# New places in the order for every step of the mixer stages MN, D and LG

## The reference

```
h = rmsnorm(x, norm1_w)
proj = h @ w_in          # mq mk mv mo mi mf nq kc vc ks vs kw vw ng gm gn
hm = mlstm_chunkwise(q, k, v, i_pre, logf)      # 4 heads
hm = rmsnorm(hm) * sigmoid(mo)
qn, kc_t, ks_t, kw_t = apply_rope(rmsnorm(...)) # 64 per head
kcmp = gelu(flat_k @ cmp_k_w1) @ cmp_k_w2       # blocks of 32 tokens, stride 16
vcmp = gelu(flat_v @ cmp_v_w1) @ cmp_v_w2
o_cmp, o_slc, o_win = nsa_branches(...)         # three softmax attentions
y = sigmoid(gm + b0) * (hm @ w_up_m) + sigmoid(gn + b1) * (on @ w_up_n)
x = x + y @ w_out
x = x + (gelu(conv(a)) * v) @ ffn_w_down        # a, v = split(rmsnorm(x) @ ffn_w_up)
```

## Time and profile before

| what | value |
|---|---|
| median of three runs | 2805.1 us (2800.53 to 2806.18) |
| profiled execution, span | 2803.7 us |
| PE busy | 2740.2 us, 98% |
| DVE, ACT, POOL busy | 65%, 46%, 18% |
| PE's share of the chain that ended last | 89% |
| MN, 98 to 420.5 us: PE busy of 322.5 | 315.75 us |
| D, 1281 to 1416 us: PE busy of 135 | 134.13 us |
| LG, 2191 to 2411 us: PE busy of 220 | 218.90 us |

### The profile page before, as it was taken

The page is one execution under the profiler, slowest core; times in us unless marked ns, Lnnn a source line. Parts: engine busy times, 40 slices in busy tenths (PEclk is TensorE's granted clock), DMA queues, the critical chain, the costliest instruction groups (busy, mean ns, idle before and its releaser), DMA issues.

```text
span 2803.7 us, 40660 instructions
## 1 busy us (share of the span) xinstructions
PE 2740.2 (98%) x15808; PEld 2348.4 (84%) x15808; DVE 1816.9 (65%) x2803; ACT 1288.7 (46%) x2190; POOL 516.9 (18%) x514
## 2 busy tenths in 40 slices
PE   8999999999999999999989999999999999899999
PEld 7787777888878898987778999889998787688988
DVE  7667666646467574756767566675765677774755
ACT  5445554322235353543644344543544686643533
POOL 1001332000003121101303212031120343131211
PEclk9999999999999999999999999999999999999999
DMA  5212104232223564631124565354653110234743
GB/s 177 66 61 93 42 27 151 90 98 98 90 83 91 142 159 129 169 109 53 31 94 134 127 166 133 122 140 113 177 130 101 42 34 28 83 96 135 191 113 113
DMA packets 112783, 296.53 MB, mean 106 GB/s; under 512 B 12624, under 2 KB 14672, under 8 KB 112336
## 3 DMA queue, kind: packets, MB, share of 16 engines
q1 hardware_dynamic: 90864, 250.80, 27.6%
q0 software_dynamic: 21152, 42.08, 9.1%
q10 hardware_dynamic: 576, 1.05, 0.1%
HBM read 291.78 MB, written 2.10 MB: 105 GB/s over the span
## 4 chain that ended last, share of the span: by engine, by line
PE 89%; DVE 6%; ACT 3%; issue 1%; POOL 0%; DMA 0%; SPq 0%; ACTq 0%; DVEq 0%; POOLq 0%
PE ps L510 87%; DVE WL L521 3%; PE ps L513 2%; ACT WH L518 1%; DVE SC L521 1%; ACT HH L518 1%; DVE X L521 1%; ACT SC L518 1%; DVE SC L533 0%; DVE HL L533 0%; POOL SC L528 0%; DMA WF<-wall 0%; DVE X2k L521 0%; DVE X2v L521 0%; DVE SM L539 0%
## 5 line engine op out<-in xcount | busy, mean ns | idle before, releaser
L521 DVE TENSOR_TENSOR WL<-WF,WH 128x1024 fp32r<-128x1024 f32 (+4 forms) x625 | 728.1, 1177 | 317.3 <-ACT WH L518 313.2
L518 ACT ACTIVATE WH<-WF 128x1024 fp32r<-128x1024 f32 (+4 forms) x625 | 581.2, 943 | 656.9 <-PE ps L510 623.0
L510 PE MATMUL ps<-HH,WH 128*128 128x512 f32 (+1 forms) x1104 | 443.5, 402 | 16.3 <-DVE HL L533 13.6
L510 PE MATMUL ps<-HH,WL 128*128 128x512 f32 (+1 forms) x1104 | 433.4, 393 | 0.0
L510 PE MATMUL ps<-HL,WH 128*128 128x512 f32 (+1 forms) x1104 | 433.1, 392 | 0.0
L510 PE MATMUL ps<-AH,WH 128*128 128x512 f32 x880 | 345.5, 393 | 19.4 <-DVE WL L521 15.6
L510 PE MATMUL ps<-AL,WH 128*128 128x512 f32 x880 | 343.3, 390 | 0.0
L510 PE MATMUL ps<-AH,WL 128*128 128x512 f32 x880 | 343.2, 390 | 0.0
L510 PE MATMUL ps<-B,WH 128*128 128x256 f32 x1632 | 299.8, 284 | 2.0 <-DVE WL L521 1.4
L521 POOL TENSOR_TENSOR SC<-SC 128x256 f32<-128x256 f32 (+2 forms) x92 | 108.2, 1182 | 983.6 <-DVE SC L533 978.7
L556 POOL DMA_DIRECT2D WF<-wall x136 | 128.8, 956 | 799.9 <-DMA WF<-wall 784.9
(11 more groups left out here) (322 smaller groups left out, 4770.7 us busy)
## 6 DMA issues: line engine op xcount, KB each, us to landing
WF<-wall SPq DMA_DIRECT2D x313, 512.0 KB, 3.8
WF<-wall SPq DMA_DIRECT2D x253, 256.0 KB, 3.0
WF<-wall POOLq DMA_DIRECT2D x136, 256.0 KB, 4.3
WF<-wall SPq DMA_DIRECT2D x40, 384.0 KB, 3.7
X<-xT POOLq DMA_DIRECT2D x8, 256.0 KB, 3.9
outT<-X POOLq DMA_DIRECT2D x8, 256.0 KB, 2.3
WF<-wall SPq DMA_DIRECT2D x4, 288.0 KB, 11.7
LT<-late POOLq DMA_DIRECT2D x1, 1152.0 KB, 5.6
```

What stands on the lines that cost most here:

```text
L510: return self.real.matmul(o, l, r, start=start, stop=stop, skip_group_check=True)
L518: return self.real.activation(o, i, func, bias=bias, scale=scale, accum_out=accum_out)
L521: return self.real.tensor_tensor(o, a, b, op) if self.real is not None else Uncounted()
```

## The change

Only the five dictionaries change: of 954 places in MN 926 differ, of 348 in D 334, of 825 in LG 798. No step is added or removed and none computes anything else. Five pairs of neighbouring weight pieces, of 625, swap places in the order in which they are fetched. The names that the prediction speaks of (the places of a stage are in the order of its keys; `source` in M has ks, kw, kc, nq0 and vc, four each; `take` and the others ks, kw, kc, nq0, and `take` also vc):

```
 M_TURNS = {
-    "source": (72, 80, 85, 86, 118, 125, 126, 147, 149, 155, 164, 165, 263, 267, 268, 269, 202, 235, 241, 253),
-    "take": (89, 152, 174, 273, 260),
-    "rot": (97, 182, 209, 275),
-    "sums": (116, 219, 234, 278),
-    "spread": (187, 236, 246, 287),
-    "done": (218, 256, 265, 316),
-    "x_made": (266, 270),
-    "x_first": (280, 282, 291, 293, 300, 303, 304, 311),
-    "x_bent": (306, 313),
-    "x_turned": (307, 320),
-    "product": (70, 145, 216, 255),
-    "h_sums": (122, 204, 225, 262),
-    "wf_low": (12, 49, 58, 101, 123, 179, 195, 274),
+    "source": (73, 80, 81, 82, 126, 129, 130, 136, 149, 150, 155, 161, 242, 248, 249, 254, 222, 224, 225, 243),
+    "take": (85, 142, 170, 267, 245),
+    "rot": (91, 173, 211, 265),
+    "sums": (138, 251, 214, 266),
+    "spread": (180, 269, 252, 301),
+    "done": (195, 290, 261, 311),
+    "x_made": (270, 246),
+    "x_first": (273, 274, 275, 281, 305, 306, 313, 314),
+    "x_bent": (292, 315),
+    "x_turned": (309, 316),
+    "product": (67, 121, 206, 244),
+    "h_sums": (109, 213, 258, 257),
+    "wf_low": (28, 69, 307, 107, 116, 187, 208, 276),
...
-    "f_part": (..., 213, 222, 264, 271),
+    "f_part": (..., 233, 259, 263, 264),
...
 D_TURNS = {
-    "made": (69, 73, 94, 131, 142, 151, 172, 177, 188, 191, 206, 239, 253, 262, 263, 296),
-    "raised": (90, 97, 102, 134, 146, 167, 179, 186, 202, 203, 217, 254, 264, 278, 295, 299),
+    "made": (82, 83, 97, 138, 148, 152, 166, 180, 193, 207, 211, 235, 257, 264, 265, 272),
+    "raised": (86, 101, 105, 140, 162, 163, 183, 184, 194, 215, 217, 262, 266, 268, 281, 296),
...
 L_TURNS = {
-    "source": (1, 6, 8, 9, 20, 43, 53, ...),
-    "take": (2, 7, 21, 26, ...),
-    "rot": (13, 19, 33, 57, ...),
+    "source": (1, 13, 5, 391, 23, 29, 56, ...),
+    "take": (3, 14, 10, 24, ...),
+    "rot": (2, 22, 18, 78, ...),
...
```

More of the change, by code:

```diff
@@ L292 @@
[L292 to L306, removed]
@@ L338 @@
[L338 to L343, removed]
@@ L344 @@
-    "half2": (534, 535, 722, 731, 839, 862, 950, 952),
-    "parts": (536, 802, 946, 953),
+    "source": (389, 390, 397, 400, 553, 554, 562, 564, 704, 705, 706, 707),
+    "ws_high": (250, 543, 683),
+    "ws_low": (147, 583, 744),
+    "take": (414, 568, 718),
+    "rot": (415, 597, 726),
+    "squares": (408, 586, 723),
+    "roped": (421, 602, 730),
+    "added": (445, 600, 743),
+    "sums": (418, 593, 748),
+    "root": (420, 594, 749),
+    "widen": (453, 601, 751),
+    "spread": (464, 610, 762),
@@ L346 @@
+    "product": (448, 465, 500, 506, 626, 634, 684, 688, 779, 781, 823, 830, 902, 910, 951, 953),
+    "half1": (517, 520, 710, 711, 857, 858, 948, 949),
+    "half2": (545, 546, 713, 728, 864, 866, 946, 947),
+    "parts": (549, 758, 950, 952),
 }
 D_TURNS = {
[L348 to L361, removed]
@@ new lines @@
+        153, 154, 164, 182, 187, 222, 224),
+    "ws_high": (15, 149, 40, 8, 62, 74, 143, 219),
+    "ws_low": (11, 298, 39, 9, 77, 116, 188, 233),
+    "take": (16, 30, 50, 75, 76, 111, 169, 230),
+    "rot": (19, 44, 81, 69, 78, 144, 185, 229),
+    "squares": (18, 37, 56, 66, 99, 110, 175, 227),
+    "roped": (32, 54, 87, 85, 96, 145, 186, 237),
+    "added": (24, 33, 79, 93, 130, 156, 197, 231),
+    "sums": (20, 38, 70, 72, 102, 115, 191, 232),
+    "root": (21, 45, 71, 73, 114, 137, 192, 234),
@@ new lines @@
+    "widen": (35, 43, 88, 84, 123, 151, 190, 238),
+    "spread": (42, 46, 117, 112, 135, 165, 228, 243),
+    "scaled": (58, 57, 129, 126, 150, 170, 236, 249),
+    "done": (53, 55, 131, 136, 168, 172, 245, 256),
+    "o_part": (59, 60, 104, 113, 128, 134, 212, 213, 250, 253, 255, 280, 293, 294, 331, 337),
+    "o_add": (61, 121, 141, 216, 260, 305, 312, 341),
+    "wo_high": (67, 108, 119, 196, 218, 263, 302, 306),
+    "wo_low": (48, 118, 132, 80, 254, 286, 311, 347),
+    "s_product": (2, 28, 0, 5),
@@ L423 @@
+    "product": (148, 216, 281, 315, 371, 425, 478, 511),
+    "half1": (169, 247, 296, 318, 408, 447, 485, 515),
+    "half2": (175, 245, 307, 328, 404, 460, 487, 525),
+    "parts": (265, 343, 479, 526),
 }
 G_TURNS = {
-    "source": (470, 471, 476, 477, 562, 564, 566, 575, 666, 671, 677, 678),
-    "ws_high": (467, 576, 659),
-    "ws_low": (488, 595, 783),
-    "take": (484, 583, 682),
-    "rot": (507, 592, 690),
-    "squares": (489, 587, 683),
-    "roped": (519, 601, 697),
-    "added": (527, 603, 709),
@@ L433 @@
-    "sums": (504, 590, 686),
-    "root": (505, 597, 700),
-    "widen": (506, 608, 701),
-    "spread": (526, 614, 708),
-    "scaled": (533, 627, 710),
-    "done": (545, 628, 715),
-    "o_part": (525, 535, 541, 542, 550, 551, 586, 600, 610, 611, 625, 650, 770, 799, 807, 813),
-    "o_add": (548, 560, 580, 609, 621, 668, 816, 819),
-    "wo_high": (485, 537, 556, 578, 615, 657, 681, 806),
-    "wo_low": (536, 558, 563, 591, 644, 702, 812, 814),
-    "made": (482, 508, 521, 522, 557, 582, 607, 624, 654, 684, 685, 707, 722, 748, 751, 768),
@@ L456 @@
-    "product": (623, 636, 695, 712, 759, 777, 810, 824),
-    "half1": (626, 637, 704, 743, 764, 796, 811, 820),
-    "half2": (634, 648, 705, 744, 766, 804, 815, 821),
-    "parts": (817, 818, 822, 823),
+    "source": (456, 469, 470, 473, 560, 561, 578, 579, 671, 672, 682, 685),
+    "ws_high": (423, 571, 661),
+    "ws_low": (458, 605, 662),
+    "take": (477, 584, 684),
+    "rot": (507, 586, 697),
+    "squares": (484, 588, 700),
+    "roped": (524, 601, 699),
+    "added": (527, 607, 693),
@@ L460 @@
+    "product": (602, 644, 694, 731, 755, 784, 805, 817),
+    "half1": (606, 632, 702, 737, 764, 785, 813, 822),
+    "half2": (630, 665, 709, 727, 781, 799, 811, 820),
+    "parts": (680, 812, 816, 823),
 }
```

274 lines of the change are left out of this document (139 added, 135 removed).

## The result

| | before | after |
|---|---|---|
| median | 2805.6 us (2800.5 to 2807.6, 4 runs) | 2787.4 us (2785.7 to 2789.0, 4 runs) |
| profiled execution, span | 2803.7 us | 2784.7 us |

The ratio is 0.994 (95% interval 0.9928 to 0.9951): 14 to 20 us less. I forecast 6 us less, to 2799.0, and a range from 2789 to 2808. The changed kernel run again later (e15) has the ratio 0.9949, which is 2791 us on the median of before and inside the range.

A forecast was written before the change was run, and what follows sets the result against it. PE, busy 98% of the span, was taken as the bound. Terms -7.3 + 1.8 + 0.8 - 1.3 - 1.65 + 2.0 - 0.7 - 0.5 gave -6.9, shaded to -6.1: 2799.0 us on the median, range 2789 to 2808.

The forecast's parts named there:

- the shade: Whole kernel: the summed gain of 6.9 us cut to 6.1, since a worked-out list misses small new waits.
- (3): LG: with fewer changes of form, one of two clock falls without a wait goes, -1.65 us; ends -3.3 and +3.3.
- (2): MN, D and LG: 33 fewer changes between 512-column pieces and short steps, half of them entries at 0.08 us, -1.3 us.
- (4): New waits at `x_turned` v 0.6, `made` (1,0) 0.6, `rot` mq0 0.8, sum +2.0; waits that go, -0.7 and -0.5 us.
- (1): MN: wait at `rot` nq0 and its clock fall go, -7.3 us; new wait ahead of `x_first` k +1.8, half a fall +0.8.
- (5): ACT in MN, D and LG: table loads from 11, 7, 17 to 15, 9, 16, some 6 us, hidden but for (4).
- more goes than I count: Rival, chance 0.15: a third of the remaining 18 us not at full pace goes besides, -12 us, ending at 2793.
- The rival that ends slower: Chance 0.15: waits at five places in MN, D and LG bring the clock down, +8.5 us, ending at 2813.6.
- the late tile of LG: LG, one of the slower rival's five places: a wait of 0.73 us at 2390.81, doubled to 1.5.

The follow-up runs named there:

- e15: The changed kernel, unchanged, run again later: 0.9949 of before.
- e1: The kernel before with only M_TURNS and N_TURNS new, and D, L and G in their old places: 0.9957 of before.
- e7: The changed kernel with gm 7's second and third piece moved from 259 and 263 to just ahead of product 3: 0.9967 of before, 2793.1 us.
- e17: The changed kernel with head 1's h_spread moved to 256.5 and its h_scaled to 299.5, behind gm 7's f_end: 0.9982 of before.
- e12: The kernel before, unchanged, profiled a second time; no ratio is given, its MN stretch took 321.6 us.
- e8: The changed kernel with head 1's h_spread moved from 234 to 256.5 and its h_scaled from 241 to 276.5: 0.9957 of before.
- e11: The changed kernel with head 1's h_spread at 256.5 and its h_scaled at 288.5, behind the low halves for x_first k: 0.9970 of before.
- e5: The kernel before with x_made v moved from 270 to 260.5 and x_made k from 266 to 273.5, PE's order untouched: 0.9999 of before.
- e6: The swap of e5 in the kernel before, with gm 7's second piece, kc's spread and head 2's sums moved behind product 3: 1.0000 of before.
- e14: The kernel before with the changed kernel's DVE and ACT order at x_made, and gm 7's second piece and kc's and kw's spreads moved there: 1.0021 of before.
- e9: The kernel before with seven M lines changed: x_made v before k, nq0's squares and take ahead of k, PE cover moved there: 0.9996 of before.
- e10: The kernel of e9 with projection piece gm 0,3 also moved from place 17 to 9.5: 0.9987 of before.
- e16: The kernel before with the x_made spot built as in the changed kernel on PE, DVE and ACT, no kw step moved: 0.9991 of before.

## Why the prediction was wrong, point by point

On the means of two profiles each, waits gave 4.5 us where my terms made 1.5, clock falls 8.5 where they made 4.15, and the rest 4.4 where I had 1.3; the shade took 0.8 more. The step that failed most is (3), the clock falls without a wait, and it is the one that differs between executions: in e15's five runs the clock gives 4.2 us, what my terms had. Forms (2) and waits (4) were priced too small by 6 us together, in the profile after as in e15's.

- **(1) The episode** was read rightly. The wait of 4.06 us went, the next one came at the place and for the releaser named, and I had 1.8 us for it where 1.40 came. `x_turned` v waits 0.5 us (forecast 0.6). I had taken half a clock fall behind it, +0.8; there was none, in the profile after nor in e15 (whose fall at 231 lies 18 us behind the end of that wait, and 2.6 behind `x_turned` v's of 0.5) nor in e1.
- **(2) Forms** was mis-sized: the rest of PE's time went down by 4.4 us (MN 1.3, D 1.0, LG 1.6 on the means above, the remainder outside), not 1.3. I had priced 33 changes of form at 0.08 us for half of them, the entries into a long step. Leaving one costs as much at some places. PE at 102.98, in the trace of before: the fp32 product behind a 512-column matmul starts 0.32 us later instead of 0.23.

```profile
102.75 0.39 PE L510 MATMUL ps<-HL,WH 128*128 128x512 f32 x1
102.98 0.39 PE L510 MATMUL ps<-HH,WL 128*128 128x512 f32 x1
103.30 0.38 PE L510 MATMUL ps<-CT,PICK 36*128 36x256 f32 x1
```

  That place is not the common one. Over the 128 undisturbed exits in the three mixers of before, the next start comes 0.033 us late on the mean and 0.005 on the median; it is late by 0.09 in 40 of them, most ahead of matmuls of 36 or 64 rows or of 64 columns. An entry costs 0.098 us on the mean. The traces have 256 changes in the three mixers before and 221 after; at these means, and at the after's own 0.028 and 0.093, that is 16.8 us before and 13.3 after. So changes of form are 3.5 of the 3.9 us that the rest lost inside the mixers; the other 0.4, and 0.5 outside them, stay open.
- **(3) Clock falls without a wait**: I priced one fall of 1.65 us less in all. Falls take 34.1 and 30.7 us in the two profiles of before and 13.7 and 17.1 in those of after, 8.5 us of time on the means; my terms for clock were -3.3, +0.8 and -1.65, that is 4.15. Of the eight places at which before had a fall I weighed four and took the others, at 106, 826, 1451 and 2448 us, as given. Three of these lie outside what the change touches, and two of the three differ after, one gone (826) and one half as long (2448). The wait of 2.19 us ahead of the stretch at 826 is the same in both kernels, with a fall behind it in one and none in the other (before, then after):

```profile
825.29 0.50 PE L510 MATMUL ps<-AH,WH 128*128 128x512 f32 x1 [2.19 <-DVE AL L521]
...
814.85 0.50 PE L505 MATMUL ps<-AH,WH 128*128 128x512 f32 x1 [2.19 <-DVE AL L516]
...
815.20:825.00 9.80, 9.80 (x45) 8.08 (x44) 6.05 (x8) 4.21 (x7) 0.00 (x0) 1.00 0.39 115
```

  The falls outside the three mixers went from 13.9 us to 6.9, so 3.5 of the 19 us between the two spans. Part of that is an execution's luck: e15 has a fall at the place of the one at 826 again. Not all of it has to be. That fall is there in all twelve profiles with the old M_TURNS or a local edit of it, and in three of the seven with the new one (e7, e15, e17). All falls outside MN take 17.1 to 23.9 us in those twelve, 20.2 on the mean, and 10.2 to 20.5 in these seven, 15.1 on the mean. How the order of MN would bear on falls hundreds of us behind it no run shows.
- **(4) New tight spots**: I counted +2.0 for them and -1.2 for waits that go. All waits together fell by 4.5 us on the means above, where my terms (-4.06, +1.8, +2.0, -1.2) made -1.5. In MN the small waits behind the episode, 0.9, 0.9, 0.5 and 0.3, were gone and one of 0.5 came, `x_turned` v's. That is 2.2 us less, where I had 0.5 less and 0.6 more. `made` (1,0) in D has no wait; the 0.69 at D's end is gone, but one of 0.57 stands at 1402. LG's waits grew from 3.1 to 4.7 us. Of the 1.6, 0.79 is the wait that I had forecast as 0.8, ahead of the rotation of mq0:

```profile
2179.22 1.07 PE L505 MATMUL ps<-SC,LT 96*96 96x512 f32 x2 [0.79 <-issue]
```

  The others are two of 0.2 and 0.3 for a low half and 0.3 more for the POOL tile. Outside the mixers waits fell by 1.3 us, which I had not looked for.
- **(5) Tables**: 59 loads instead of 57, 13, 10 and 15 in the three stretches where I had 15, 9 and 16; none ended in a wait of PE that the profile names. Hidden, as said.
- **The shade** of 0.8 us, for small waits that working through a list misses, had the wrong sign: what the list missed was on the side of the gain.

Of the rivals, "more goes than I count", at 0.15, is what happened, and it ended at 2793 where the median is 2787.4. The rival that ends slower needed waits and falls at five places; one of the five had a wait above 1.2 us, and the clock stayed up behind it. Its sum also counts the late tile of LG at its full 1.5 us, though 0.73 of that was there before, so it should have ended at 7.8 and not 8.5. And its sentence on the Trainium skill drew more from that section than stands there: the waits told of there are longer than any of the five, so by it alone this case is not the likelier.

## What to carry to other kernels

Where PE is 98% busy, look for what busy hides: sum the time at the lower clock over the whole span and halve it, beside the waits. Price a change by both and by its changes of form on both sides, and give the range the spread of falls between two profiles of the same kernel. A spot with a long step on one engine must be checked against the queues of all engines that it passes; five of my six local rebuilds failed on a step in a queue that the edit had not looked at. And take no fall of a single profile as evidence for an edit until the unchanged kernel has been profiled twice.

## What the hardware showed that I had not expected

The unchanged kernel had its clock falls at different places and of other lengths in two executions: 3.4 us at 106 and 6.8 at 219 in one, none and 10.2 in the other, 10.2 us in sum in both. Behind one and the same wait of 2.2 us, in the same code at about 825 us, the clock fell in some executions (before, e12, e15 and twelve more) and not in others (after, e1, e8, e11). Behind a wait of 3.9 to 4.6 us at the `x_made` spot it fell in each of the profiles listed here that had one (before, e12, e5, e6, e7, e14). Shorter waits did not rule it out: it fell at those of 2.9 to 3.1 us in e9, e10 and e16 and at the 1.89 of e8. The two profiles' waits in MN were the same to a tenth of a us. The times of before on one chip, 27 runs, spread over 8.5 us (2801.7 to 2810.2); clock falls make up most of this spread: the two runs with a granted clock of 0.993 have 2808.0 us on the mean, the 20 with 0.994 have 2805.0, the five with 0.995 have 2803.3.
